# Second block: projections dealt in pieces of three products, another order of growth, softmax weighting shared between VectorE and ScalarE

## The reference, cut to what matters

```python
h = rms_norm_2(x, norm_pre[layer])
(gq, gk, gv, gg, gaf, gab, dq, dk, dv, dg, hq, hzf, hzb, hi, hg) = jnp.split(h @ w_in[layer], offs, axis=-1)
y_a = gla_branch(...)    # gated scan, both directions, 4 heads of 32 keys
y_b = diff_branch(...)   # differential attention, 4 heads
y_c = hgrn_branch(...)   # gated scan, both directions, 4 heads of 64 keys
x = x + rms_norm_2(jnp.concatenate([y_a, y_b, y_c], axis=-1) @ w_out[layer], norm_post[layer])
```

```python
s = jnp.einsum('cbhqd,cbhkd->cbhqk', qblk, k)      # c: two score maps
p = jax.nn.softmax(s, axis=-1)
w = p[0] - lam * p[1]
return jnp.einsum('bhqk,bhkv->bhqv', w, v)
```

## Time and profile before

| | |
|---|---|
| median of 3 runs | 4527.01 us (4520.32 to 4527.04) |
| profiled execution | 4519.45 us |
| its span | 4517.6 us |
| mean granted TensorE clock | 0.927 |
| PE busy | 3900.1 us (86%) |
| DVE busy | 2015.4 us (45%) |
| ACT busy | 1438.9 us (32%) |
| POOL busy | 957.7 us (21%) |

### The profile page before, as it was taken

How to read it: one execution, slowest core, us unless ns; L and a number is a source line. 1 busy time by engine, 2 the same in 40 slices (tenths; PEclk the granted TensorE clock), 3 DMA queues, 4 the chain that set the end, 5 groups by cost and what they waited for, 6 DMA issues and landing times.

```text
span 4517.6 us, 66477 instructions
## 1 busy us (share of the span) xinstructions
PE 3900.1 (86%) x29096; PEld 2414.5 (53%) x29396; DVE 2015.4 (45%) x2163; ACT 1438.9 (32%) x1795; POOL 957.7 (21%) x426
## 2 busy tenths in 40 slices
PE   6988899999989999988996978978687978978677
PEld 3555565666656665455443555555453555555454
DVE  3456455545454542423124354263633254264542
ACT  4222323233232322222013323433443223343442
POOL 2313333232233322031131201111002200111002
PEclk8999999999999999999998978999898989989889
DMA  2111111111111112432222100100011100100002
GB/s 92 53 38 39 48 43 49 44 48 49 39 53 39 62 44 84 172 125 85 107 70 76 34 10 11 42 15 29 19 57 67 34 15 5 42 19 19 24 16 92
DMA packets 61585, 226.93 MB, mean 50 GB/s; under 512 B 6832, under 2 KB 8560, under 8 KB 60784
## 3 DMA queue, kind: packets, MB, share of 16 engines
q1 hardware_dynamic: 50064, 181.77, 11.5%
q10 hardware_dynamic: 11232, 40.90, 2.3%
HBM read 174.93 MB, written 47.71 MB: 49 GB/s over the span
## 4 chain that ended last, share of the span: by engine, by line
PE 70%; DVE 16%; ACT 9%; issue 2%; DMA 1%; POOL 1%; ACTq 0%; DVEq 0%; SPq 0%; POOLq 0%
PE psum L932 69%; DVE arena L1991 6%; ACT arena L1486 5%; DVE arena L1994 5%; DVE arena L2434 2%; DVE arena L2371 2%; PE psum L935 2%; ACT L1486 1%; ACT wh L1486 1%; DMA arena<-in_w_proj_conv 1%; DVE arena L1998 1%; ACT arena L1932 1%; DVE hl L1991 1%; POOL arena L2483 0%; POOL wl L2483 0%
## 5 line engine op out<-in xcount | busy, mean ns | idle before, releaser
L932 PE MATMUL psum<-arena 64*64 64x32 f32 (+12 forms) x19108 | 1593.2, 283 | 406.4 <-ACT arena L1486 173.6
L932 PEld LDWEIGHTS psum<-arena 64*64 64x64 f32 (+6 forms) x19108 | 1111.6, 159 | 896.2 <-issue 444.6
L932 PE MATMUL psum<-hh,wh 128*128 128x512 f32 x3120 | 896.5, 433 | 104.9 <-DVE arena L1994 27.9
L2483 POOL TENSOR_TENSOR wl<-arena,wh 128x1024 bf16<-128x1024 f32 (+1 forms) x195 | 474.6, 2434 | 2394.1 <-ACT wh L1486 2392.1
L1486 ACT ACTIVATE arena<-psum 128x512 f32<-128x512 f32 (+4 forms) x660 | 415.8, 630 | 1389.1 <-PE psum L932 1049.9
L932 PEld LDWEIGHTS psum<-hh,wh 128*128 128x128 f32 x3120 | 609.0, 201 | 309.6 <-issue 61.7
L932 PE MATMUL psum<-hh,wl 128*128 128x512 bf16 (+1 forms) x2910 | 741.9, 395 | 22.2 <-issue 7.3
L1991 DVE TENSOR_TENSOR arena<-psum,arena 128x512 f32<-128x512 f32 (+3 forms) x488 | 319.4, 655 | 978.7 <-PE psum L932 637.1
L932 PE MATMUL psum<-hl,wh 128*128 128x512 bf16 (+1 forms) x3030 | 715.2, 382 | 15.4 <-issue 8.2
L1994 DVE SCALAR_TENSOR_TENSOR arena<-arena 128x1024 f32<-128x1024 f32 x348 | 564.5, 1622 | 83.7 <-ACT arena L1486 70.8
L2483 POOL TENSOR_TENSOR arena<-arena 128x1024 f32<-128x1024 f32 (+4 forms) x142 | 361.8, 2548 | 959.9 <-ACT arena L1486 468.6
(11 more groups left out here) (34 smaller groups left out, 856.8 us busy)
## 6 DMA issues: line engine op xcount, KB each, us to landing
arena<-in_w_in SPq DMA_DIRECT2D x161, 512.0 KB, 3.5
scr_g<-arena ACTq DMA_DIRECT2D x24, 512.0 KB, 2.6
arena<-scr_g SPq DMA_DIRECT2D x24, 512.0 KB, 4.4
arena<-in_w_out SPq DMA_DIRECT2D x24, 512.0 KB, 3.5
arena<-in_w_mem_kv SPq DMA_DIRECT2D x16, 512.0 KB, 3.5
scr_x<-arena SPq DMA_DIRECT2D x16, 512.0 KB, 2.6
arena<-scr_x SPq DMA_DIRECT2D x16, 512.0 KB, 7.3
arena<-in_x SPq DMA_DIRECT2D x8, 512.0 KB, 10.4
```

The lines of the kernel that those rows point to most:

```text
L932: return pe.e.matmul(o, l, r, start=start, stop=stop)
L2483: return pool.seq.tensor_tensor(o, a, b, op)
```

## The change

A yield may now carry a share, which is what is taken off the units owed (1 if it has none). The projections of `dv_ready`, `qk_ready` and `head_out` are cut into pieces of 3 products at a share of 0.25, where they were pieces of 12 at 1. The yields after the copies and rotations count 0.5. `beside` is stepped twice per yield of the attention with BESIDE/12, and the table BESIDE is new. `weave` hands the share of the main generator on to the filler's step. The scan's own projections keep pieces of 12.

The growth is issued as keys of both directions, queries of both, trees of both. `xk` and `kt` wait for the second key product, `lev` for the second query product.

The weighting, which was one step of four DVE operations, is now three steps. `dr` (DVE) takes the reciprocals and the lambda factor; `e1` (ACT) scales the first exponentials, queued behind `WT` of the block before; `dw` (DVE) adds the second ones, one yield later, after `e1`.

```diff
 class Filler:
     def step(self, n=1.0):
         self.owed += n
         while self.owed >= 1 and self.live:
-            self.owed -= 1
             try:
-                next(self.g)
+                self.owed -= next(self.g) or 1
...
 def weave(main, *fillers):
-    for stage in main:
-        for f, *n in fillers:
-            f.step(n[min(stage or 0, len(n) - 1)])
+    for share in main:
+        for f, n in fillers:
+            f.step(n * (share or 1))
...
     def dv_ready(L, h):
-        yield from P(("dvp", L, h), A["w_in_2"][L][14 + h], f"p{L}", deep=4)
+        yield from P(("dvp", L, h), A["w_in_2"][L][14 + h], f"p{L}", deep=1, share=0.25)
         do("dv_copy", L, h)
-        yield
+        yield 0.5
         two(("dv_turn", L, h), ("dv_turn", L, h))
...
         if n < 32:
-            do("dw", L, h, q)
+            do("dr", L, h, q)
         yield
         if n:
             for g in range(2):
                 do("WT", L, *last, g)
+        if n < 32:
+            do("e1", L, h, q)
         yield
+        if n < 32:
+            do("dw", L, h, q)
         if n:
             one(("dv", L, *last), ("dv", L, *last), UPPER)
...
-    BESIDE = ((1, 2, 3, 2, 3, 3, 3, 2), (5, 6, 4, 3, 0, 0, 1, 6), (3, 4, 3, 4, 3, 1, 0, 0), (0, 2, 3, 3, 3, 2, 2, 0))
+    BESIDE = ((1, 1.9, 2.1, 2.1, 2.1, 2.2, 2.4, 2.6), (5, 5, 4, 3, 0, 0, 4, 4), (3, 3, 3, 3, 2, 1, 1, 1.4), (1, 2, 3, 3, 3, 2, 2, 0))
...
             for _ in attend(L, n):
                 ahead.step(pace[h])
-                other.step(BESIDE[h][q] / 6)
+                other.step(BESIDE[h][q] / 12)
                 ahead.step(pace[h])
+                other.step(BESIDE[h][q] / 12)
...
+        def e1(L, h, q):
+            z = q % 2
+            act.wait_ge(*at("dr", L, h, q))
+            f(EX[z], EX[z], AF.Copy, scale=DST[:, 16 * z + 6:16 * z + 7]).then_inc(*act.up("e1", L, h, q))
...
             m = 1 << lv
+            T, n = [tree(d, lv) for d in range(2)], 512 >> lv
             for d in range(2):
-                T = tree(d, lv)
-                tt(half(KG[d], d, m), half(KG[d], d, m), T[:, :, 1 - d:2 - d].to_broadcast([128, 512 >> lv, m]), MUL).then_inc(*dve.up("grow_k", L, t, lv, d))
-                tt(half(QF[d], 1 - d, m), half(QF[d], 1 - d, m), T[:, :, d:d + 1].to_broadcast([128, 512 >> lv, m]), MUL).then_inc(*dve.up("grow_q", L, t, lv, d))
-                x = tt(tree(d, lv + 1, True).unsqueeze(2), T[:, :, 0:1], T[:, :, 1:2], MUL)
-                x.then_inc(*dve.up(*(("grow", L, t, lv) if d else ("grow_0", L, t, lv))))
+                k = half(KG[d], d, m)
+                tt(k, k, T[d][:, :, 1 - d:2 - d].to_broadcast([128, n, m]), MUL).then_inc(*dve.up("grow_k", L, t, lv, d))
+            for d in range(2):
+                q = half(QF[d], 1 - d, m)
+                tt(q, q, T[d][:, :, d:d + 1].to_broadcast([128, n, m]), MUL).then_inc(*dve.up("grow_q", L, t, lv, d))
+            for d in range(2):
+                tt(tree(d, lv + 1, True).unsqueeze(2), T[d][:, :, 0:1], T[d][:, :, 1:2], MUL).then_inc(*dve.up("grow_t", L, t, lv, d))
...
-        def dw(L, h, q):
+        def dr(L, h, q):
             z = q % 2
             s = DST[:, 16 * z:16 * z + 16]
             dve.wait_ge(*at("dexp", L, h, q, 1))
             dve.seq.reciprocal(s[:, 6:8], s[:, 4:6]).then_inc(*dve.up("dw_rec", L, h, q))
-            tt(s[:, 8:9], s[:, 7:8], sc[:, 4:5], MUL).then_inc(*dve.up("dw_lam", L, h, q))
-            ts(EX[z], EX[z], s[:, 6:7], None, MUL).then_inc(*dve.up("dw0", L, h, q))
+            tt(s[:, 8:9], s[:, 7:8], sc[:, 4:5], MUL).then_inc(*dve.up("dr", L, h, q))
+
+        def dw(L, h, q):
+            z = q % 2
+            s = DST[:, 16 * z:16 * z + 16]
+            dve.wait_ge(*at("e1", L, h, q))
             stt(EX[z], EX[2], s[:, 8:9], EX[z], MUL, ADD).then_inc(*dve.up("dw", L, h, q))
```

More of the change, by code:

```diff
@@ L329, in do, with P @@
         plan.append(step)
-    def P(key, src, h, n=S, m=128, back=False, among=LOWER, deep=2):
+    def P(key, src, h, n=S, m=128, back=False, among=LOWER, deep=2, share=None):
         PROJ[key] = (src, h, n, m, back)
@@ L337, in P @@
         for part in range(steps // deep):
-            yield
+            yield share
             if part == 0:
@@ L768, in qk_ready @@
         for i in range(2):
-            yield from P(("dqk", L, h, i), A["w_in_2"][L][6 + 4 * i + h], f"p{L}", deep=4)
+            yield from P(("dqk", L, h, i), A["w_in_2"][L][6 + 4 * i + h], f"p{L}", deep=1, share=0.25)
             do("dq_copy", L, h, i)
-            yield
+            yield 0.5
             held(("rope", L, h, i), ("rope", L, h, i))
-            yield
+            yield 0.5
             do("turned", L, h, i)
@@ L783, in head_out @@
         ps.leave(("do_sum", L, h))
-        yield from between(P(("dg", L, h), A["w_in_2"][L][18 + h], f"p{L}", deep=4), None, ("do_norm", L, h))
+        yield from between(P(("dg", L, h), A["w_in_2"][L][18 + h], f"p{L}", deep=1, share=0.25), None, None, None, ("do_norm", L, h))
         ps.keep(("proj", ("dg", L, h)), 2)
@@ L1303, in lev @@
                 else:
-                    pe.wait_ge(*at("grow", L, t, lv - 1))
+                    pe.wait_ge(*at("grow_q", L, t, lv - 1, 1))
             for c in range(4 * g, 4 * g + 4):
@@ L1316, in kt @@
             cleared(use)
-            pe.wait_ge(*at("grow", L, t, 6))
+            pe.wait_ge(*at("grow_k", L, t, 6, 1))
             for c in range(4 * g, 4 * g + 4):
```

9 lines of the change are left out of this document (4 added, 5 removed).

## The result

The changed kernel takes 4501.27 us (median of 4 runs, 4497.40 to 4503.67) where the one before takes 4523.66 on the same chip (4518.82 to 4527.04): a ratio of 0.995, with a 95% interval of 0.9933 to 0.9968. That is 22 us less, where 82 were forecast. The sign was right and the size was not. The range held the time only because it reached from the much faster rival to the one without change: the forecast's own case ended at 4490.

A forecast was written before the change was run, and what follows sets the result against it. PE's order of work was taken as the bound, with gaps waiting for DVE and ACT. Terms -18 - 38 - 12 + 14 - 6 - 22 = -82 took 4519.45 to 4437, plus 7.6 gave 4445 us; range 4365 to 4530.

The forecast's parts named there:

- the forecast's own case: Whole kernel: the summed terms hold, 4445 us, spanning 4400 to 4490; chance 0.60.
- Finer dealing: Second block's attention: small pieces cover `leve` waits, -38 us (bounds +20, -85), other waits -12, copies laid bare +14.
- the -22 of the clock: Scan level stretches: a third of idle time goes, granted clock rises, -22 us (bounds 0 and -60).
- The price of the pieces: After projections: PSUM copies exposed in half of 24 places, pair kept longer, +14 us (bounds 0 and +26).
- Growth order: Between scan levels: `xk` and level wait only for their own products, -18 us (bounds 0 and -37).
- Softmax weighting: Attention blocks: one scaling per block moves from DVE to ACT, -6 us (bounds +40 and -48).
- Rival 1: Weighting: DVE stands for ACT's scaling ahead of `dw`, delaying `leve` and growth; slower, 4547 at half the blocks; chance 0.14.
- Rival 2: Scan levels: one PSUM pair left, growth order gains nothing, dealing's gain returns as other waits; -2 us, 4525; chance 0.11.
- the signs: Level gaps 165 to under 110 us, `xk` 1.4 us after growth's start, first-stretch clock above 0.8, 649-us stage 30-50 shorter.
- Rival 3: Scan stretches: PE becomes dense, 110 us of gaps and 45 of clock go; much faster, 4372 us; chance 0.15.

The follow-up runs named there:

- dealing alone: The kernel before with only the finer, more even dealing (pieces of 3, new shares, new BESIDE): 4575.47 us, ratio 1.0114.
- growth with weighting: The changed kernel with the dealing of before, keeping the new growth order and softmax weighting: 4503.28 us, ratio 0.9953.
- the cut subtractions: GpSimd's subtraction for the second block's input weights cut to 128 of 1024 columns: kernel before 4517.79 us; with the finer dealing as its only other change 4550.21 us.
- late on DVE: New growth, weighting all on VectorE, scaled and summed at the late place: 4515.38 us with the new dealing, 4512.61 us with the old.
- Growth alone: The kernel before with only the growth in the new order: 4517.79 us, ratio 0.9987.
- The shared kernels: New growth, weighting late and shared between VectorE and ScalarE: ratio 0.9950 with the new dealing (the changed kernel), 0.9953 with the old.
- the early place: The changed kernel with ScalarE's scaling and the sum right behind the reciprocals: 4617.28 us, ratio 1.0213.
- moving `leve` forward: The changed kernel with fine dealing in the last head only (4488.36 us), then the last `leve` put between the growth's keys and queries: 4499.19 us.

## Why the prediction was right or wrong

**Finer dealing: the step that failed.** It was put at -38 - 12 + 14, and most of the -22 of the clock hung on it. The runs give +52 us alone and about 0 with the other parts. The step took half of the 71.0 us that `leve` releases. That share rose to 94.4 after, and stayed in the first layer with dealing alone, 38.5 for 37.8. The closest comparison is growth with weighting, whose level gaps are 141.6 us with 71.4 of them released by `leve`: the dealing added 23 us where it was to take 36 away, and PE's idle time in all grew by 16. The step's error was to price a gap as one `leve` of 1.3 us. I had named the rest (DVE 70% busy, work standing before `leve`), but only as a discount of one half. Where 2 us of weighting stand ahead of `leve`, the dealing costs 48 us in place of gaining; with the weighting out of the way it costs 8 or nothing. That a cover of 0.85 us everywhere is worse there than 2.8 us at times is my reading of the single rows above. The upper bound of +20 for this term was too tight as well, because rows 8 and 9 were read one by one and no stretch was followed for what stood ahead of each `leve`. Of the 52 us, some 19 are collisions with GpSimd by the cut subtractions. The place of the weighting gives 47 us in the kernel with the new growth, and not by fewer collisions (with it late on DVE they have 32.0 us of excess a layer against 25.8), so the two don't simply add; their split isn't settled.

**The price of the pieces (+14)** is borne out in the trace. The stretch ahead of the attention has 34 of 380 weight loads less and lasts 99.1 us for 100.7. Its idle time rose from 10.9 to 15.8 us, 4.9 a layer, and copies are laid bare there: the gaps ahead of rotations went from 0.2 to 5.0 us, and 1.7 came ahead of the first scores. This is 10 us in all ahead of the attention; inside it, gaps ahead of rotations rose from 6.5 to 9.8 us in the first layer, and those ahead of projections from 12.8 to 19.4.

**Growth order (-18)** gave -6 (-10 to -2): the mechanism was right and the term too large. The order of time after, at 2681 us, shows both halves:

```profile
2680.95 3.52 DVE L2000 TENSOR_TENSOR arena<-arena 128x512 f32<-128x512 f32 x6
2682.45 1.29 ACT L1490 ACTIVATE arena<-arena 128x512 f32<-128x512 f32 x2 [10.25 <-DVE arena L2000]
...
2684.51 1.31 DVE L2380 COPY_PREDICATED arena<-arena,psum 128x1024 f32<-128x1024 int32 x1
...
2685.87 2.08 PE L936 MATMUL psum<-arena 32*128 32x128 f32 x16 [6.24 <-DVE arena L2380]
```

`xk` starts 1.5 us after the growth's start, as forecast (1.4), and is done at 2683.74; the level starts at 2685.87, when `leve` has freed the pair. Growth alone shows the same in its groups, first layer:

```profile
L932 PE MATMUL psum<-arena 32*128 32x128 f32 x512 | 45.8, 340 | 28.4 <-DVE arena L2371 20.0 <-ACT arena L1486 6.0 <-DVE arena L1991 2.3
L932 PE MATMUL psum<-arena 64*128 64x128 f32 x512 | 45.8, 328 | 46.8 <-DVE arena L2371 22.2 <-ACT arena L1486 16.2 <-DVE arena L1991 5.0
```

ACT's release fell by 14.8 us against rows 4 and `leve`'s rose by 4.4; the gaps fell by 7.0 a layer. I took half of the ceiling of 37; 14 went from the gaps, and 6 from the time.

**Softmax weighting (-6)** gave -15 (-19 to -10) alone. ACT's scaling takes 1.15 us, where 1.08 was taken, and DVE is busy 52 us less in that kernel (1963.4). I had priced the engines and not the place: with the new growth and the old dealing the late place gives 6 and the sharing 9. The rule that sends the multiplication to VectorE (the Trainium skill, "ScalarE: Activation LUTs", section "Rules for kernel authors") would have made this part a loss, as the prediction worked it out. The shared kernels are 9 and 19 us faster than those with all of it late on DVE, so in this kernel it doesn't pay to follow it.

So the other terms together came to about +8 us in place of -60: not the clock but the idle time is what wasn't won. Growth with weighting shows it too: it is as fast as after at 0.928, with 20 us more of PE's busy time and 16 us less of idle time. So the clock's share of the forecast did come with the dealing, and its idle time went the other way.

**Rival 1** came half true. After, DVE stands for ACT ahead of `dw` and its like, first layer:

```profile
L2003 DVE SCALAR_TENSOR_TENSOR arena<-arena 128x1024 f32<-128x1024 f32 x38 | 55.4, 1459 | 70.6 <-ACT arena L1490 68.2
```

The weighting's 32 operations are among the 38. By the trace 15 of them wait for ACT, 13 for over 1 us, the mark that I had set, and yet the kernel is faster. The wait is new: the 42.1 us of the earlier trace rows stood ahead of four other operations (the longest of them 14.08 us at 3153.03), and the scaling itself followed the reciprocals at once, as at 2646.77 to 2647.17. What these waited for ACT's exponentials was 25.3 us before and is 36.8 after, so that didn't go away either. 12 of the 15 waits lie outside the scans' levels, where no `leve` is queued behind; in the early place 14 lie inside (4617 us). The prediction's case against this rival also took a block at 20 us, by a stage of 649; the four heads last 812 us, so a block has 25. **Rival 2** is nearest to what dealing does in the changed kernel: the gaps changed their releaser and the sum is nil. Its mechanism, one pair left, is in rows such as the one at 2685.87, but moving `leve` forward didn't help. As for the signs: the level gaps fell to 144.2 us and not under 110, ACT's share of them fell and DVE's rose, the clock of the first head rose from 0.79 to 0.85, and the four heads of the first layer last 801 us in place of 812, where the stage was to shorten by 30 to 50. **Rival 3** fell.

## What to carry to other kernels

Before work is dealt more finely to cover a wait, follow one whole period and write down what stands ahead of the releasing instruction on its own queue: here a thin even cover hid one short operation and not three. Move what isn't urgent behind the instruction that another engine waits for, before moving it to another engine; here the place was worth 47 us with fine pieces and the other engine 19. Parts of such a change aren't additive, so run each alone and each left out: the largest part of this one was worth nothing, and kept to the last head it was worth 18 us. And split every difference into PE's busy and idle time before explaining it by waits; twice here (the dealing, the moved `leve`) the two went opposite ways.

## What the runs showed of the hardware that was not expected

DVE operations with two sources in SBUF are lengthened when they meet GpSimd's TENSOR_TENSOR: 1.28 to 3.46 us beside 2.35. Operations that read from PSUM weren't: 24 of the predicated copies and reductions meet one after, and none is longer. Who starts first decides. Of after's scalar_tensor_tensor operations of 128x1024 with both inputs in SBUF 123 meet one. All 67 that began after GpSimd's are longer, and each ends 1.08 to 1.09 us after it. Of the 56 that began before, 44 kept their time, and GpSimd's ended 1.8 to 2.3 us after them; the 12 others had begun less than 0.05 us ahead, as the one at 3205.30 had. The Trainium skill, "SBUF — State Buffer", section "SBUF: two separate sides", says that the two engines share one pair of ports, which whoever starts first has for the whole instruction, and counts DVE operations with two SBUF inputs against a GpSimd operation that reads SBUF. The trace agrees, but for those 12. Averages hide it: DVE's busy share is 43 to 46% in all kernels, while the excess is 2 to 32 us a layer in those with whole subtractions, by how the plan happens to lay the two engines' work. Cutting GpSimd's subtractions gave 7 us in one order and 26 in the other.

The granted clock doesn't follow a stretch's idle share. In head 0 of before PE is busy for 154.51 of 193.90 us, in head 3 of after for 147.44 of 185.40, both 80%; the clocks are 0.79 and 0.94.
